# One block-pipelined output stage: where two of the four row transposes and router products of each block stand in TensorE's order

## The reference

```python
out = jnp.einsum('btc,cd->btd', jnp.concatenate([o, u], axis=-1), w_out)
...
x = x + gt1 * mix
h = _rmsnorm(x, norm_ffn_g) * (1.0 + sc2) + sh2
x = x + gt2 * _ec_moe(h, w_router, w_e_gate, w_e_up, w_e_down)
...
logits = jnp.einsum('btd,de->bte', h, w_router).astype(jnp.float32)
aff = jax.nn.softmax(logits, axis=-1)
gate, idx = lax.top_k(jnp.swapaxes(aff, 1, 2), cap)
```

## Time and profile before

| | |
|---|---|
| median of three runs | 2720.18 us |
| the profiled execution, its time / its span | 2712.45 us / 2709.8 us |
| its mean granted TensorE clock | 0.927 |
| PE / DVE / ACT / POOL busy | 91% / 60% / 45% / 29% |
| stage 3 on PE: first product to last router product | 863.3 us to 1322.5 us |

### The profile page before, as it was taken

The page is one execution under the profiler, slowest core; times in us unless marked ns, Lnnn a source line. Parts: engine busy times, 40 slices in busy tenths (PEclk is TensorE's granted clock), DMA queues, the critical chain, the costliest instruction groups (busy, mean ns, idle before and its releaser), DMA issues.

```text
span 2709.8 us, 41042 instructions
## 1 busy us (share of the span) xinstructions
PE 2461.4 (91%) x15405; PEld 2166.3 (80%) x15405; DVE 1624.5 (60%) x2729; ACT 1208.0 (45%) x1946; POOL 782.2 (29%) x686
## 2 busy tenths in 40 slices
PE   5679989999997889999649999999999999999994
PEld 1667868688785566777418999999999999999994
DVE  0575949679496453342464666665566666665575
ACT  3555355464423233323115555555544555555553
POOL 1020010101000031101012554445555544445451
PEclk9879989999997879889658999999999999999997
DMA  5884565665545446432444766667777666666875
GB/s 194 304 289 159 172 214 190 232 199 183 198 164 204 132 140 163 121 113 84 128 87 141 207 194 191 192 184 205 198 199 206 194 195 195 183 196 198 285 230 202
DMA packets 287074, 505.61 MB, mean 187 GB/s; under 512 B 31614, under 2 KB 230107, under 8 KB 271098
## 3 DMA queue, kind: packets, MB, share of 16 engines
q1 hardware_dynamic: 247562, 377.84, 42.4%
q0 software_dynamic: 39408, 126.38, 17.8%
HBM read 405.63 MB, written 98.53 MB: 186 GB/s over the span
## 4 chain that ended last, share of the span: by engine, by line
PE 77%; DVE 6%; ACT 4%; DMA 3%; issue 2%; POOL 2%; SPq 0%; DVEq 0%; ACTq 0%; POOLq 0%
PE bank L1423 22%; PE bank L1425 22%; PE bank L1424 22%; PE bank L1606 2%; PE bank L1544 1%; DVE work_out L2079 1%; PE bank L1672 1%; PE bank L1637 1%; PE bank L1583 1%; PE bank L1571 1%; DVE work_exp L2272 1%; ACT work_proj L747 1%; PE bank L1663 1%; DMA out_dram<-work_exp 1%; PE bank L1484 1%
## 5 line engine op out<-in xcount | busy, mean ns | idle before, releaser
L1423 PE MATMUL bank<-act_hl_exp,hl_exp 128*128 128x288 f32 x3072 | 913.0, 297 | 38.3 <-POOL act_hl_exp L1341 25.3
L1424 PE MATMUL bank<-act_hl_exp,hl_exp 128*128 128x288 f32 x3072 | 909.2, 296 | 0.0
L1425 PE MATMUL bank<-act_hl_exp,hl_exp 128*128 128x288 f32 x3072 | 907.5, 295 | 0.0
L1423 PEld LDWEIGHTS bank<-act_hl_exp,hl_exp 128*128 128x128 f32 x3072 | 579.0, 188 | 42.0 <-issue 30.3
L1425 PEld LDWEIGHTS bank<-act_hl_exp,hl_exp 128*128 128x128 f32 x3072 | 581.3, 189 | 0.0
L1424 PEld LDWEIGHTS bank<-act_hl_exp,hl_exp 128*128 128x128 f32 x3072 | 580.2, 189 | 0.0
L2390 DVE TENSOR_TENSOR hl_exp<-work_exp,hl_exp 128x1024 fp32r<-128x1024 f32 x192 | 231.7, 1227 | 226.4 <-ACT hl_exp L1030 226.4
L2390 DVE TENSOR_TENSOR hl_exp<-raw_exp,hl_exp 128x1024 fp32r<-128x1024 f32 x192 | 232.3, 1225 | 201.9 <-ACT hl_exp L1030 201.9
L2032 DVE SCALAR_TENSOR_TENSOR work_proj<-work_proj,wcv 128x392 f32<-128x392 f32 (+11 forms) x600 | 343.2, 644 | 0.0
L1030 ACT ACTIVATE hl_exp<-work_exp 128x1024 fp32r<-128x1024 f32 x192 | 199.5, 1055 | 217.8 <-PE bank L1425 212.6
L1030 ACT ACTIVATE hl_exp<-raw_exp 128x1024 fp32r<-128x1024 f32 x192 | 198.6, 1052 | 166.4 <-PE bank L1425 166.4
(11 more groups left out here) (320 smaller groups left out, 3642.8 us busy)
## 6 DMA issues: line engine op xcount, KB each, us to landing
hl_proj<-park_w POOLq DMA_DIRECT2D x80, 1024.0 KB, 5.5
raw_exp<-in_w_e_gate_dram SPq DMA_DIRECT2D x32, 1024.0 KB, 5.7
raw_exp<-in_w_e_up_dram SPq DMA_DIRECT2D x32, 1024.0 KB, 5.7
work_exp<-in_w_e_gate_dram SPq DMA_DIRECT2D x32, 1024.0 KB, 6.2
work_exp<-in_w_e_up_dram SPq DMA_DIRECT2D x32, 1024.0 KB, 5.8
raw_exp<-in_w_e_down_dram SPq DMA_DIRECT2D x32, 1024.0 KB, 5.6
work_exp<-in_w_e_down_dram SPq DMA_DIRECT2D x32, 1024.0 KB, 5.7
park_w<-hl_proj SPq DMA_DIRECT2D x10, 2048.0 KB, 12.5
```

The source lines that it names most:

```text
L1423: pe.matmul(out, lh, rh, start=first, stop=False)
L1424: pe.matmul(out, lh, rl, start=False, stop=False)
L1425: return pe.matmul(out, ll, rh, start=False, stop=last_)
```

## The change

Tiles with `late(g)` are the third tiles of blocks 1 to 3: g = 4, 8 and 12.

- Third tile: its transposes move from between the halves of the fourth tile to behind the second half. Its router product moves from behind the fourth tile to between the halves of the next block's first tile. Since its old bank is then in use by that tile's output, it takes bank 2((g + 1) % 2), the bank of the fourth tile's first half; so it waits for `residual` of the fourth tile to have read that half.
- Last tile: its transposes move from between the halves of the next block's first tile to behind the second half; its router product from ahead of `conv_mean` to between `conv_mean` and `inter`. It waits for the late tile's logits, whose bank it shares.
- DVE reads the logits accordingly: the late tile's after `inverse(g0 - 1)` of the next block, the last tile's after `centre`.
- In block 4 (tiles 14 to 17), nothing is prepared. Its first steps take the new order; its third tile keeps the old one.

```diff
+        def late(g):
+            return 0 < M_OF[g] < NBLK and g - G3[M_OF[g]] == 2
+        def logit_bank(g):
+            return 2 * ((g + 1) % 2) if late(g) else 2 * (g % 2)
...
                     if q == 0:
-                        pe.wait_ge(r_lg, g - 1)
+                        wait_pos(pe, r_lg, g - 2 if late(g - 2) else g - 1)
...
             def router(g):
                 pe.wait_ge(r_ev, 2 * g + 2)
-                pe.wait_ge(r_y, 2 * g + 1)
+                pe.wait_ge(r_y, 2 * (g + 1 if late(g) else g) + 1)
+                if late(g - 1):
+                    pe.wait_ge(r_lg, g)
...
             def stage3(m):                      # PE
                 out_half(g0, 0)
+                if m > 1:
+                    router(g0 - 2)
+                out_half(g0, 1)
                 if m > 0:
                     row_T(g0 - 1)
-                out_half(g0, 1)
+                if prep:
+                    conv_mean(prep)
                 if m > 0:
                     router(g0 - 1)
                 if prep:
-                    conv_mean(prep)
                     inter(prep)
...
                 out_half(g0 + 3, 0)
-                row_T(g0 + 2)
+                if not prep:
+                    row_T(g0 + 2)
                 out_half(g0 + 3, 1)
-                router(g0 + 2)
+                if prep:
+                    row_T(g0 + 2)
+                else:
+                    router(g0 + 2)
...
                     inverse(g0 - 1)             # DVE
+                if m > 1:
+                    logit(g0 - 2)
                 if prep:
                     back_states(prep, 4, NC3[prep])
+                    centre(prep)
                 if m > 0:
                     logit(g0 - 1)
                 if prep:
-                    centre(prep)
                     add_inter(prep)
...
                 inverse(g0 + 2)
-                logit(g0 + 2)
+                if not prep:
+                    logit(g0 + 2)
```

More of the change, by code:

```diff
@@ L1668, in router @@
                 pe.wait_ge(r_ev, 2 * g + 2)
-                pe.wait_ge(r_y, 2 * g + 1)
+                pe.wait_ge(r_y, 2 * (g + 1 if late(g) else g) + 1)
+                if late(g - 1):
+                    pe.wait_ge(r_lg, g)
                 c = 0 if M_OF[g] == 0 else 1
                 for k in range(KC):
-                    last = pe.matmul(psum[2 * (g % 2)][:, 0:NE], h2T[:, g % 2, k, :], wrA[:, c, k, :], start=(k == 0),
+                    last = pe.matmul(psum[logit_bank(g)][:, 0:NE], h2T[:, g % 2, k, :], wrA[:, c, k, :], start=(k == 0),
                                      stop=(k == KC - 1))
@@ L2150, in logit @@
                 dve.wait_ge(r_ro, g + 1)
-                dve.tensor_tensor(logits[:, ROW3[m] // 128 + g - G3[m], :], psum[2 * (g % 2)][:, 0:NE],
+                dve.tensor_tensor(logits[:, ROW3[m] // 128 + g - G3[m], :], psum[logit_bank(g)][:, 0:NE],
                                   brow[:, 0 if m == 0 else 1, :], ALU.add).then_inc(r_lg, 1)
```

## The result

The changed kernel took 2679.35 us (median of 4 runs, 2672.05 to 2693.52), the kernel before on the same chip 2717.53 us (4 runs, 2705.38 to 2720.66). The ratio is 0.9877, with a 95% interval from 0.9851 to 0.9903. The profiled execution took 2680.78 us, where my sum said 2691.1.

A forecast was written before the change was run, and what follows sets the result against it. PE was taken as the bound, with holes in stage 3; savings of 8.32 + 6.30 + 6.30 + 0.45 = 21.4 us took 2712.45 to 2691.1, or 2699 us on the median, range 2691 to 2710.

The forecast's parts named there:

- Block 1's hole: Wait before tile 1's transposes in block 1's first tile: 6.55 us was to shrink to 1.1 us.
- ahead of the transposes of tiles 4, 5, 8, 9 and 12: Sign of being right: PE's waits there, such as 1.28 and 3.39 us at edge 1/2, would vanish.
- 0.85 before a head: PE's wait for `centre` ahead of head 1 of the state products, 0.85 us, was to go.
- ahead of tile 13's router product: Edge of blocks 3 and 4: a new hole of 1.2 us, waiting for ACT's copies with no means between.
- the second case: Rival: `park_c` lands late for the means, 4.2 us in block 1, 2.3 in two others; 2707.6 us, chance 0.16.
- The third case: Rival: stage 3's saving is not handed on past its end; 2720 us, chance 0.06.
- Rule and row: DVE's 16 state steps beside POOL's two low parts: 2.0 us later by the trace; by the rule, POOL could lose.
- TensorE's clock: Half clock around the state products: taken as zero change, plus or minus 2 us per block.
- more than forecast: full clock through heads 1 to 3: Rival: state products stay at full clock, up to 3 us more per block; 2690 us, chance 0.05.
- the *longer* stretch between two half tiles: Transposes, means, router product before the state products: an earlier half clock might cost 1.5 us in head 0, 1.74 in router.

The follow-up runs named there:

- e12_after_fill: Changed kernel with the last tile's router product moved between heads 0 and 1 of the state products; 2692.10 us against 2711.91 for the kernel before, ratio 0.9923.
- e1: The kernel before, unedited, profiled a second time; 2727.59 us beside 2732.79 for itself, ratio 0.9987.
- e5: Changed kernel with only DVE's order altered: logits read ahead of centring, restoring head 1's hole; 2707.45 us against 2733.73 for the kernel before.
- e7: Kernel before with only the third tile's part of the change; 2718.01 us against 2733.73, ratio 0.9946.
- e9: Kernel before with the last tile's router product moved between heads 0 and 1 of the state products; 2742.60 us against 2748.52, ratio 0.9975.
- e4: Changed kernel with the last tile's router product put back ahead of the means; 2707.11 us against 2732.79 for the kernel before, ratio 0.9908.
- e2: The changed kernel, unedited, second profile; 2696.94 us against 2732.79 for the kernel before, ratio 0.9882.
- e3: Kernel before with only the last tile's router product moved between means and state products, DVE likewise; 2717.07 us against 2732.79, ratio 0.9937.
- e6: Changed kernel without the third tile's part, so only the last tile's part; 2707.48 us against 2733.73 for the kernel before, ratio 0.9903.
- e8: Changed kernel with tile 13's transposes put back between tile 14's halves; 2698.43 us against 2733.73 for the kernel before, ratio 0.9883.
- e11: The changed kernel, unedited, third profile; 2706.51 us against 2748.52 for the kernel before, ratio 0.9859.
- e14: Repeat of e3, the kernel before with only the router product moved between means and state products; 2698.59 us against 2711.91, ratio 0.9946.
- e13: Kernel before with the change's other steps and all four heads between the second tile's halves; 2677.67 us against 2711.91, ratio 0.9866.

## Why the prediction was wrong

**Right by its steps.** Block 1's hole left 1.17 us (1.1 forecast). There is none ahead of the transposes of tiles 4, 5, 8, 9 and 12, none of 0.85 before a head in blocks 1 to 3, and 1.17 us ahead of tile 13's router product. `park_c`, the second case, was never late: at edge 1/2 it was issued at 1051.67 and landed in 4.6 us, 4.4 us before the means at 1060.68. The third case fell too: the stage's 32.0 us are the executions' 2712.45 - 2680.78 = 31.7. As a sum, e12_after_fill comes to 21.7 us against 21.4, and that is in part luck: by stretches it is 7.3, 7.7 and 9.2 us less against 8.3, 6.3 and 6.3 forecast, and from tile 11 to the end 2.5 us more instead of 0.45 less. What bears the steps out are the single holes.

**Rule and row.** 16 state steps beside POOL's two parts were to lose 2.0 us by the row. They took 6.82 us instead of 4.74, 2.08 more, and this cost PE nothing. POOL's parts:

```profile
1048.94 2.70 POOL L1246 TENSOR_TENSOR cat_hl<-work_out,cat_hl 128x512 fp32r<-128x512 f32 x2 [8.02 <-ACT cat_hl L939]
```

1.35 us each, against 1.26 without such neighbours: nearly all of the loss is DVE's. The Trainium skill (SBUF — State Buffer, "Who interferes with whom") has the two exclude each other; for DVE's side the trace agrees, and POOL as the loser isn't shown by any run here.

**The step that failed: TensorE's clock, "I take zero and keep plus or minus 2 us per block".** It was the case "more than forecast: full clock through heads 1 to 3", to which I gave 0.05 and 3 us a block. Both were too small. Where the clock holds, the heads take 7.15 us instead of 11.26, 4.1 less; the half tile behind them 5.7 instead of 6.8 to 8.0, 1.1 to 2.3 less; and the next transposes then wait 0.6 to 1.6 us for ACT, since nothing of ACT's has become faster. That is some 4.6 to 5 us a block net. It held in six of nine blocks of the changed kernel. 21.4 + 2 x 5 makes 31.4; measured were 32.0 in the first pair of profiles and 34.0 in the means. The price was there in the earlier trace rows: three heads at head 0's 1.89 us make 5.7, 3.7 less than their 9.37, before anything is added for the half tile behind them. Two smaller terms of the clock were missing too and nearly cancel: a `spread` took 6.5 to 6.7 us in five of six blocks before and 5.0 in eight of nine after, and the half tile behind the new hole took 1.6 us more.

What I had read wrong was the row itself. I saw heads 1 to 3 at half clock in the earlier trace rows and took this for a property of these products; the question was what stood ahead of them. The forecast asked only whether the *longer* stretch between two half tiles would lower the clock sooner. I priced the hole of 0.85 us at 0.85 us, and the router product's new place at nothing.

**What the runs show, and what they don't.** In blocks 1 to 3, with something thin *among* the 64-column products, be it a hole of 0.83 us or the 16-column router product, no block of 18 kept the clock (before, e1, e5, e7, e9, e12); in e4, with the hole and a second one earlier, one of three did. With the router product beside the means instead, and nothing among the heads, 14 of 21 did (after, e2, e3, e6, e8, e11, e14). With half tiles directly on both sides three of three did (e13).

These blocks are not independent draws. In each profile all rises and falls of the granted clock in stage 3, 20 to 36 of them, lie on one even beat, to within 0.01 us, and from one execution to the next the blocks lie differently to it. That sorts the 21 blocks with nothing thin among the heads without an exception. Take the first beat that comes more than 1 us behind the start of head 0. In seven blocks it came at 1.2 to 2.1 us, and there the clock fell on it; in 14 it came at 2.85 to 3.9 us, and the clock held. So the one block in three that falls is the one where a beat lies early in the heads, and the order of PE alone doesn't settle it.

So a thin spot has to be judged between blocks at the same place:

- **Hole and order together.** The kernel before, e1 and e7 have the beat at 3.55 to 3.76 us in six blocks, and all six fell. e3 and e14 have it at 3.71 to 3.87 in four, and all four held, as did e6's three and e8's block 1 at 3.33 to 3.79.
- **The hole alone.** e5's block 3 fell at 2.90 us; the changed kernel held in four blocks with the beat at 2.85 to 2.89. e5's block 1, at 2.12, is no evidence, since e8 fell at 2.09 without a hole; its block 2, at 2.60, has no counterpart.
- **The router product among the heads alone.** In e12 what stands ahead is shorter, so count from the start of the transposes: block 2 fell at 9.12 us, and e2 held at 9.11 and 9.12. Block 1, at 8.03, is no evidence, since the changed kernel fell at 7.8 to 8.0; block 3, at 8.56, has no counterpart.

The effect of the two together is thus shown by six blocks against eight. Each by itself is shown by one block against its counterparts, and the size that the hole or the router product has alone isn't shown. Nor is a thin spot a certain loss: with a hole among the heads, five blocks 0 of 16 and e4's block 2 kept the clock. In these six it had risen 0.55 to 1.2 us before head 0; in the seven blocks where it had risen 1.3 to 2.0 us before, it fell again.

The Trainium skill (TensorE: Matmul & The Clock Gate, "Part 1: The HAM clock gate") has the clock follow how busy PE has been of late, as a monitor sees it that runs freely and doesn't start anew with the kernel, and so has the same kernel come out differently from run to run. The direction agrees with all of these runs, and the beat of the changes with the free running.

## What to carry to other kernels

A short wait or a thin product amid narrow matmuls can cost several times its length if TensorE's clock falls there, so read the granted clock of each stretch beside the idle time, and ask of slow products what stood ahead of them. Put narrow products (router, transposes) next to dense ones, not among other narrow ones. When PE gets faster in one place, look for the next hole where another engine had been just in time; and compare kernels over several profiles, since single blocks of one program differ by 5 us, and compare blocks where the clock's changes could come at the same place in them.

## What the hardware showed that I had not expected

- 0.83 us idle ahead of 48 products of 64 columns: they took 10.50 us, without it and at full clock 5.4. In the stage it was 13.5 us for 2.5 us of holes, of which the fall in block 1 isn't the hole's.
- It needs no idle time. With 16 products of 16 columns (1.9 to 2.1 us) in the same place, six blocks of six fell. And in block 3 of the changed kernel's first profile the clock fell at 1150.6, in the heads, with no hole of over 0.1 us on PE since 1118.1.
- The changes of the granted clock lie on one even beat, and where it met the heads sorted 21 blocks of 21.
- A longer hole need not do harm: in e3_swap's block 2 the 3.39 us ahead of tile 5's transposes stand, and behind them a half tile, means, router product and heads all ran at full clock (heads 7.1 us). A shorter one can: behind the 1.17 us ahead of tile 13's router product the next half tile took 7.2 us in all three profiles of the changed kernel.
